# Output projections as split column halves, with columns of x turned between them, in a two-block language model

## The reference

```python
h = h + recurrent_block(...)      # ... return (y * hr) @ w_out
h = h + swiglu(h, ...)            # width 2816
h = h + nsa_layer(...)            # ... return o.reshape(B, S, N_HEADS * HEAD_DIM) @ w_out
h = h + swiglu(h, ...)
for layer in range(2):
    x = x + hybrid_mixer(rms_norm(x, ...), ...)   # return jnp.einsum('bsd,de->bse', y, w_out)
    x = x + swiglu_2(rms_norm(x, ...), ...) if layer % 2 == 0 else x + moe_swiglu(...)   # width 3584
return rms_norm(x, g)

def swiglu(h, norm_g, w_in, w_out):
    u = rmsnorm(h, norm_g)
    gu = u @ w_in
    return (jax.nn.silu(gu[..., :FFN_HIDDEN]) * gu[..., FFN_HIDDEN:]) @ w_out
```

## Time and profile before

| | us |
|---|---|
| median of 3 runs | 2581.16 (2578.05 to 2584.66) |
| the profiled execution | 2593.58 |
| its span in the trace | 2592.0 |
| PE busy (share of the span) | 2433.8 (94%) |
| DVE busy | 1652.1 (64%) |
| ACT busy | 1338.6 (52%) |

### The profile page before, as it was taken

One profiled execution on the slowest core, in us unless ns is written; L12 is line 12 of the kernel. 1 busy time (PEld: TensorE's weight loads), 2 busy tenths in 40 slices (PEclk: granted clock), 3 DMA queues, 4 the chain that ended last, 5 costly groups with the idle time before them and its releaser, 6 DMA issues.

```text
span 2592.0 us, 30679 instructions
## 1 busy us (share of the span) xinstructions
PE 2433.8 (94%) x12234; PEld 1975.8 (76%) x12234; DVE 1652.1 (64%) x1472; ACT 1338.6 (52%) x1184; POOL 58.6 (2%) x68
## 2 busy tenths in 40 slices
PE   7899998998998999899989988999999999999998
PEld 6488845767888896788789866777777877778876
DVE  5255535526546654555575557788878888888877
ACT  3244303425435663433457525666666667666765
POOL 0000010000000000000000001000000000000010
PEclk9999998999999999999999999999999999999999
DMA  6275363006553323555333237999999999999995
GB/s 217 82 259 194 132 229 114 1 17 240 180 182 106 131 98 130 195 194 194 138 130 130 98 138 286 348 358 357 356 345 357 368 363 362 368 354 374 369 375 213
DMA packets 251090, 588.53 MB, mean 227 GB/s; under 512 B 6476, under 2 KB 14864, under 8 KB 251008
## 3 DMA queue, kind: packets, MB, share of 16 engines
q1 hardware_dynamic: 244160, 564.27, 59.8%
q0 software_dynamic: 6656, 23.04, 2.4%
q10 hardware_dynamic: 192, 0.05, 0.0%
HBM read 573.19 MB, written 14.16 MB: 227 GB/s over the span
## 4 chain that ended last, share of the span: by engine, by line
PE 60%; DMA 16%; DVE 12%; ACT 9%; issue 2%; SPq 0%; ACTq 0%; DVEq 0%; PEldq 0%
DMA raw<-in_moe_w_gate 13%; PE ps L583 10%; PE ps L585 10%; PE ps L584 10%; DVE wl L1638 7%; PE ps L539 7%; ACT wh L1191 7%; PE ps L892 3%; PE ps L894 3%; PE ps L893 3%; DMA raw<-in_moe_w_down 2%; PE ps L531 2%; PE ps L838 1%; PE ps L794 1%; PE ps L779 1%
## 5 line engine op out<-in xcount | busy, mean ns | idle before, releaser
L1638 DVE TENSOR_TENSOR wl<-raw,wh 128x4096 fp32r<-128x4096 f32 (+1 forms) x221 | 968.9, 4386 | 246.6 <-ACT wh L1191 246.2
L1191 ACT ACTIVATE wh<-raw 128x4096 fp32r<-128x4096 f32 (+1 forms) x221 | 796.1, 3603 | 471.5 <-PE ps L585 187.5
L583 PE MATMUL ps<-wh,xmh 128*128 128x512 f32 x896 | 360.5, 402 | 34.2 <-DVE wl L1638 13.4
L584 PE MATMUL ps<-wl,xmh 128*128 128x512 f32 x896 | 352.7, 394 | 0.0
L585 PE MATMUL ps<-wh,xml 128*128 128x512 f32 x896 | 352.6, 394 | 0.0
L583 PE MATMUL ps<-wh,hh 128*128 128x512 f32 x712 | 279.5, 393 | 13.4 <-DVE hl L1653 13.3
L585 PE MATMUL ps<-wh,hl 128*128 128x512 f32 x712 | 278.0, 390 | 0.0
L584 PE MATMUL ps<-wl,hh 128*128 128x512 f32 x712 | 277.8, 390 | 0.0
L583 PE MATMUL ps<-wh,xh 128*128 128x512 f32 (+1 forms) x632 | 247.3, 391 | 17.5 <-issue 14.3
L584 PE MATMUL ps<-wl,xh 128*128 128x512 f32 (+1 forms) x632 | 243.1, 385 | 0.0
L585 PE MATMUL ps<-wh,xl 128*128 128x512 f32 (+1 forms) x632 | 243.1, 385 | 0.0
(11 more groups left out here) (477 smaller groups left out, 3378.4 us busy)
## 6 DMA issues: line engine op xcount, KB each, us to landing
raw<-in_moe_w_gate SPq DMA_DIRECT2D x56, 2048.0 KB, 9.7
raw<-in_moe_w_up SPq DMA_DIRECT2D x56, 2048.0 KB, 9.6
raw<-in_moe_w_down SPq DMA_DIRECT2D x56, 2048.0 KB, 9.5
raw<-in_w_in SPq DMA_DIRECT2D x22, 2048.0 KB, 8.0
raw<-in_f_w_in SPq DMA_DIRECT2D x20, 2048.0 KB, 8.4
raw<-in_f_w_out SPq DMA_DIRECT2D x10, 2048.0 KB, 8.1
raw<-in_dense_w_gate SPq DMA_DIRECT2D x7, 2048.0 KB, 7.7
raw<-in_dense_w_up SPq DMA_DIRECT2D x7, 2048.0 KB, 8.2
```

The source lines that it names most:

```text
L583: mm(ps[:, bank, 0:n], xa, a, start=(begin and k == 0), stop=False)
L584: mm(ps[:, bank, 0:n], xa, l, start=False, stop=False)
L1191: fn(wh[:, kind, 0:n], raw[:, s, 0:n], ACT.Copy).then_inc(wh_full[kind], 1)
L1638: v.tensor_tensor(wl[:, kind, 0:n], raw[:, plan[name][kind][0], 0:n], wh[:, kind, 0:n].bitcast(F32), ALU.subtract).then_inc(wl_full[kind], 1)
```

## The change

A new order for the four output products and what follows them:

- All four sites are split products in quarters of 256 columns, by one function (out_project on each engine). Sites 0 and 1 were full products. The banks of PSUM are 3, 4 and 5 (ring g), and wmo and ul have places in SBUF that live through all four sites.
- The operand of site 0 is made in halves: DVE multiplies, ACT copies to uh, DVE subtracts to ul. In the attention DVE copies each pair of heads to uh and subtracts it to ul, in place of the copy to oT.
- The first two quarters of the weights are split early: at site 0 between two evictions of ACT, and at site 1 in the first step of the attention.
- While a site multiplies quarter q + 1, DVE adds quarter q to x, and PE then turns these columns of x (turn_columns), which ACT and DVE split into xh and xl. The first gate and up tiles of the network behind it are split in between.
- The barriers in front of the three networks are gone. The first products of the network are ordered by k: four of gate's eight k, the last turn, and then the rest as the columns are ready; up is begun before gate ends where the tile has 256 columns.

Before, ACT had only the L1413 rows (then L1319) there. The diff, cut to what the steps need:

```diff
+                self.g = Ring([3, 4, 5], x_filled, x_added)
...
+        SITES = [(("a_out",), "ffn0", "f_norm", 0), (("b_out",), "ffn1", "f_norm", KD),
+                 (("mix_out", 0), "ffn2", "ffn_norm_2", 0), (("mix_out", 1), None, None, None)]
...
+            def natural(b, wh_, wl_):
+                for m in range(M):
+                    for k in range(KD):
+                        o, ms = ps[:, b, m * HW:(m + 1) * HW], slice(m * P, (m + 1) * P)
+                        mm(o, uh[:, k, ms], wh_[:, k, :], start=(k == 0), stop=False)
+                        mm(o, uh[:, k, ms], wl_[:, k, :], start=False, stop=False)
+                        t = mm(o, ul[:, k, ms], wh_[:, k, :], start=False, stop=(k == KD - 1))
+                return t
+            def turn_columns(site, q):
+                pe.wait_ge(x_added, 4 * site + q + 1)
+                b = me.s.claim(pe)
+                for kk_ in range(2):
+                    for m in range(M):
+                        t = tr(ps[:, b, (kk_ * M + m) * P:(kk_ * M + m + 1) * P],
+                               x[:, m, (2 * q + kk_) * P:(2 * q + kk_ + 1) * P], ident)
+                t.then_inc(s_filled, 1)
+            def out_project(site):
+                for q in range(4):
+                    me.see(mh_ready)
+                    me.see(ml_ready)
+                    b = me.g.claim(pe)
+                    natural(b, wmo[:, q % 2], out_view(site, q, raw_low)).then_inc(x_filled, 1)
+                    out_used[site, q] = (x_filled, me.g.n)
+                    if q % 2:
+                        released(out_key(site, q), me.g)
+                    if q and SITES[site][1]:
+                        turn_columns(site, q - 1)
...
-            me.see(yh_ready)
-            for t in range(2):
-                arrived(pe, ("a_out", t))
-                for m in range(M):
-                    product(me.v, ("a_out", t), m, rg)
-                released(("a_out", t), me.v)
             drained(me.v)
+            drained(me.a)
+            me.see(ul_ready, 2)
+            out_project(0)
...
-                norm(split="raw")
+                site = [s[1] for s in SITES].index(name)
+                def first_tile():
+                    def filled(kind):
+                        pe.wait_ge(wh_full[kind], B0 + 1)
+                        pe.wait_ge(wl_full[kind], B0 + 1)
+                    def split_columns(q):
+                        pe.wait_ge(s_read, me.s.n - 3 + q)
+                    filled(0)
+                    pe.wait_ge(s_read, me.s.n - 1)
+                    first_product(0, U0, w0, range(0, 4))
+                    turn_columns(site, 3)
+                    split_columns(2)
+                    first_product(0, U0, w0, range(4, 6))
+                    if w0 < FB:
+                        filled(1)
+                        first_product(1, U0, w0, range(0, 6))
+                    split_columns(3)
+                    first_product(0, U0, w0, range(6, KD)).then_inc(g_done, 1)
+                    if w0 == FB:
+                        filled(1)
+                    first_product(1, U0, w0, range(6 if w0 < FB else 0, KD)).then_inc(u_done, 1)
...
-            for t in range(2):
-                arrived(pe, ("b_out", t))
-                for m in range(M):
-                    product(me.v, ("b_out", t), m, oT)
-                released(("b_out", t), me.v)
-            drained(me.v)
-            me.barrier("ffn1")
+            drained(me.a)
+            drained(me.o)
+            out_project(1)
...
-                for t in range(2):
-                    for c in range(2):
-                        half_natural(me.v, Q_OUT + 2 * t + c)
-                    released(("mix_out", layer, t), me.v)
                 drained(me.v)
+                out_project(2 + layer)
...
+            def high_out(site, q):
+                arrived(act, out_key(site, q))
+                if q > 1:
+                    act.wait_ge(*out_used[site, q - 2])
+                fn(wmo[:, q % 2], out_view(site, q), ACT.Copy).then_inc(mh_ready, 1)
...
+            def high_columns(site):
+                b = me.s.take(act)
+                for kk_ in range(2):
+                    k = 2 * j + kk_
+                    t = fn(xh[:, k, :], ps[:, b, kk_ * S:(kk_ + 1) * S], ACT.Copy, scale=col(g, off + k))
+                t.then_inc(norm_h, 1)
+            def out_project(site):
+                name = SITES[site][1]
+                high_out(site, 2)
+                if not name:
+                    high_out(site, 3)
+                    return
+                nb, w0, B0, U0 = FFN[name]
+                high(name, 0, 0, U0, KD * w0)
+                high_columns(site)
+                high_out(site, 3)
+                high_columns(site)
+                high(name, 1, 0, U0, KD * w0)
...
+                if f in (3, 5):
+                    high_out(0, f // 2 - 1)
             act.wait_ge(a_read, me.a.n)
             act.nop().then_inc(yg_ready, 1)
+            for j in range(2):
+                me.see(yh_ready)
+                fn(uh[:, 4 * j:4 * j + 4, :], rg[:, 4 * j:4 * j + 4, :], ACT.Copy).then_inc(uh_ready, 1)
...
+            high_out(1, 0)
             probs(0, *pairs[0])
+            high_out(1, 1)
...
+            def low_out(site, q):
+                me.see(mh_ready)
+                v.tensor_tensor(out_view(site, q, raw_low), out_view(site, q), wmo[:, q % 2].bitcast(F32),
+                                ALU.subtract).then_inc(ml_ready, 1)
+            def add_columns(q):
+                b = me.g.take(dve)
+                xs = x[:, :, q * HW:(q + 1) * HW]
+                v.tensor_tensor(xs, xs, ps[:, b, :].rearrange("p (m n) -> p m n", m=M), ALU.add).then_inc(x_added, 1)
+            def low_columns(site):
+                b = me.s.take(dve)
+                me.see(norm_h)
+                for kk_ in range(2):
+                    k = 2 * j + kk_
+                    t = v.scalar_tensor_tensor(xl[:, k, :], ps[:, b, kk_ * S:(kk_ + 1) * S], col(g, off + k),
+                                               xh[:, k, :].bitcast(F32), ALU.mult, ALU.subtract)
+                t.then_inc(s_read, 1)
+            def out_project(site):
+                name = SITES[site][1]
+                add_columns(0)
+                low_out(site, 2)
+                if not name:
+                    add_columns(1)
+                    low_out(site, 3)
+                    add_columns(2)
+                    add_columns(3)
+                    return
+                nb, w0, B0, U0 = FFN[name]
+                n0 = KD * w0
+                low(name, 0, B0, n0)
+                low_columns(site)
+                add_columns(1)
+                low_out(site, 3)
+                low_columns(site)
+                add_columns(2)
+                if w0 < FB:
+                    low(name, 1, B0, n0)
...
+                add_columns(3)
+                low_columns(site)
+                low_columns(site)
+                if w0 == FB:
+                    low(name, 1, B0, n0)
...
-            link(v.tensor_tensor_scan(rg[:].rearrange("p k t -> p (k t)"), aa[:].rearrange("p k t -> p (k t)"),
-                                      ig[:].rearrange("p k t -> p (k t)"), 0.0, ALU.mult, ALU.add))
+            parts = [slice(0, KD // 2), slice(KD // 2, KD)]
+            for p_ in parts:
+                link(v.tensor_tensor_scan(rg[:, p_, :].rearrange("p k t -> p (k t)"), aa[:, p_, :].rearrange("p k t -> p (k t)"),
+                                          ig[:, p_, :].rearrange("p k t -> p (k t)"), 0.0, ALU.mult, ALU.add))
+            low_out(0, 0)
+            low_out(0, 1)
             me.see(yg_ready)
-            v.tensor_tensor(rg[:], rg[:], yg[:], ALU.mult).then_inc(yh_ready, 1)
-            for t in range(2):
-                for m in range(M):
-                    residual(t, m)
+            for p_ in parts:
+                v.tensor_tensor(rg[:, p_, :], rg[:, p_, :], yg[:, p_, :], ALU.mult).then_inc(yh_ready, 1)
+            for p_ in parts:
+                me.see(uh_ready)
+                v.tensor_tensor(ul[:, p_, :], rg[:, p_, :], uh[:, p_, :].bitcast(F32), ALU.subtract).then_inc(ul_ready, 1)
...
-                    v.tensor_copy(oT[:, h // 2, m * P:(m + 1) * P], ps[:, b, 0:P]).then_inc(o_read, 1)
+                    o = slice(m * P, (m + 1) * P)
+                    link(v.tensor_copy(uh[:, h // 2, o], ps[:, b, 0:P]))
+                    v.tensor_tensor(ul[:, h // 2, o], ps[:, b, 0:P], uh[:, h // 2, o].bitcast(F32),
+                                    ALU.subtract).then_inc(o_read, 1)
             me.scores_begin()
             maxima(0, *pairs[0])
+            low_out(1, 0)
+            low_out(1, 1)
...
-            po.wait_ge(stage, 3 * marks["ffn1"])
+            po.wait_ge(d_done, FFN_END["ffn1"])
```

178 lines of the change are left out of this document (74 added, 104 removed).

## The result

The changed kernel takes 2560.71 us (median of 4 runs, 2559.39 to 2569.71), the kernel before 2582.91 beside it (4 runs, 2578.05 to 2586.65). The ratio is 0.9921, 95% interval 0.9895 to 0.9947: 22.2 us faster. I had forecast 10.7 us less, 2570.5, with a range of 2563 to 2579, which the median misses by 2.3 us. In the two profiled executions the spans are 2592.0 and 2568.1 us, 23.9 apart. Two later sets gave ratios of 0.9905 (0.9875 to 0.9935) and 0.9916 (0.9882 to 0.9949).

What follows compares the result with a forecast made beforehand. Before 1550 us PE's chain of work plus its waits was taken to bound each stage. Savings of 5.0 (site 0), 2.3 (site 1 with attention) and 3.4 (site 2) make 10.7, off 2581.16: 2570.5 us, range 2563 to 2579.

Steps and rivals of the forecast that it cites:

- site 0, net of its later start: First product to first hb at site 0: 43.6 us falls to 33.5, less later start and half rate; 5.0 saved.
- site 1, entry: First product to first hb at site 1: 43.7 us falls to 33.5, less 0.9 for half rate; 9.3 saved.
- attention: first step, other heads, end: Attention before site 1: 4.2 us stall in first step, 2.5 in first-half heads, 0.3 behind last head; 7.0 lost.
- site 2: First product to first hb at site 2: 49.1 us falls to 45.7, half rate included; 3.4 saved (1.0 to 5.8).
- site 3: Last site, before the routing: order kept and the routing's barrier stays, so 0 us saved (within 0.3).
- half-rate terms: PE at 1.2 GHz after waits: 1.7 us at site 0's start, 0.9 each at sites 0 and 1, 2.4 at site 2.
- my sign of a wrong prediction: A stretch from the routing on differing by more than 3 us would make the prediction wrong.
- added subtraction: Attention's odd heads: copy plus dependent subtraction, 0.31 us more each; 2.5 in the first token half, 0 in the second.
- New waits: Rival, 25%: new waits eat the gain, each of three sites paying 2 us more; 4.7 us left, 2576.5.
- drain of 1.4 us: Rival, 2%: ACT drains at table switches; sites 0 and 1 lose 2.8 us each, site 2 1.4; 2577.5.
- Deeper gain: Rival, 16%: no half rate after short waits and heads absorb the added subtraction; about 15 us saved, 2566.
- the slower case: Rival, 5%: longer diagonal waits keep PE at 1.2 GHz in attention's first token half; some 19 us lost, 2589.

Runs made afterwards that it cites:

- after_wait: The changed kernel with 20 products ahead of site 3 whose result is thrown away (17.2 us in all); median 2575.49 us.
- The best version: The changed kernel with attention's early splits spread, site 0 begun on ul's first half, squares split, silu's table loaded behind the root; medians 2553.48 and 2552.51 us.
- before_ul: The kernel before with ul 128 bytes lower in SBUF, where the changed kernel has it; median 2576.67 us against 2584.55, ratio 0.9977.

## Why the prediction was wrong

The mechanisms were right in the main, and each size of the plan can be set beside its measurement, in us saved between the two profiled executions:

| step | forecast | measured |
|---|---|---|
| site 0, net of its later start | 5.0 | 6.1 |
| site 1, entry | 9.3 | 11.4 |
| attention: first step, other heads, end | -7.0 | -6.1 (-4.0, -1.7, -0.5, rounded) |
| site 2 | 3.4 | 5.0 |
| site 3 | 0 | 1.9 |
| rest of networks and mixers | 0 | -1.0 |
| routing to the end | 0 | 6.6 |
| sum | 10.7 | 23.9 |

- **The step that failed is the term put at nothing, "Site 3 keeps its order ... 0 (within 0.3)", and beside it the sizes of the terms for sites 0 to 2, all too low.** Site 3 gained 1.9 us in all three profiles. I took the order of instructions for all that counts, and passed over lines of the diff that move ul by 128 bytes. With ul moved back site 3 takes 30.7 us again, and with ul moved in the kernel before it takes 28.8; some 0.4 of the 1.9 us are the pace, the rest is the clock of the first quarter, which went with the place wherever nothing else had been changed ahead of site 3. Why it does is open. The place also made my quarters too dear: I took 0.120 us a product from rows of the old place, and it was 0.118, 0.4 us a site.
- **No single term carries the shortfall.** Up to the routing the forecast fell 6.5 us short (17.2 measured): site 1 by 2.1, site 3 by 1.9, site 2 by 1.6, site 0 by 1.1, the attention by 0.9, less 1.0 for the rest of networks and mixers. With site 3 at 1.9 the sum would have been 12.6 and the forecast 2568.6. The other two profiles have the routing 19.0 and 22.3 us earlier than before.
- **The half-rate terms were of the right kind and partly of the wrong size.** I charged sites 0 and 1 with 0.9 us each for the wait for silu; there PE lost none. Nor did it behind the waits inside site 2 (granted clock 1.00), for which I had 2.4. Ahead of the first quarters it did lose: at site 0, where I had 1.7, 27, 15 and 27 products ran at 1.2 GHz in the three profiles (2.6 and 1.4 us), and at site 2, where the rows of before held 1.7, 27 or none. The bounds held all of these; which value an execution takes is luck.
- **The stage of the experts was taken as equal.** "Differs by more than 3 us" from the routing on was my sign of a wrong prediction, and it came true (6.6). But this stage takes 1022.8 to 1036.2 in three profiles of one kernel, and arriving as late as before did not lengthen it (after_wait). The best version, with the new order and the new place of ul, took 1041.7, as long as before. In the medians it still seems shorter: 22 to 25 us of difference against 17 to 22 at the routing, and the two profiles of the old order have 1041.7 and 1039.2, where the fifteen of the new order have 1021.8 to 1041.7, 1031.7 in the mean. Whether some us of that have a cause stays open.
- **What held:** silu as the last releaser at sites 0 and 1; the waits of 1.49 and 2.77 us at site 2 (1.3 and 2.9); 4.0 us in the attention's first step (4.2); the barriers' removal cost nothing visible; the next tile of weights was in time (PE's later wait is 3.0 us, as in the earlier trace rows). From DVE's multiplication to PE's first product at site 0 it took 2.6 us longer in all three profiles (2.5 forecast), though the start itself came 0.7 to 3.4 us later, since what lies ahead of it varies.
- **What was right for another reason.** I had the added subtraction in the attention's first 16 heads (2.5 us) and none in the second 16. The first took 0.8 us longer (2.0 against before_ul) and the second 0.9, in all three profiles: the second half did not have the slack that I gave it.
- **The rivals.** New waits did not eat the gain: the margin before the fourth quarter at sites 0 and 1 held, and PE shows no wait there. The first half of the attention did not stay at 1.2 GHz: its granted clock was 0.90, as before (0.89). No drain of 1.4 us stands behind a table load: root and silu start 0.01 to 0.02 us after theirs. "Deeper gain" (2566) was the nearest, for a part of its reason: no half rate after the short waits. Its other half, heads that absorb the subtraction, was not so (1.7 us paid).
- **Slips in the sums.** A third of the growth of 57.6 us by 0.89 / 0.5 is 15 us and not 19, so the slower case lay at 2585.5, not at 2589, and under the bound of 2588.9; and site 2's lower end is 5.8 - 4.4 = 1.4, not 1.0. Neither moves the forecast or the range.

## What to carry to other kernels

Read a diff for what it moves in SBUF as well as for what it moves in time, and before an edit is credited with a gain, look at the pace of one instruction form that the edit should leave alone. When work is moved off a path, follow the next engine's chain to its end, table loads and the waits that stand ahead of them included: that chain gave the last 1.2 us of site 1. Where an edit changes how long an engine idles ahead of a stage, read more than one profile before the stage's time is credited to the edit. Keep a stage that waits for transfers out of the comparison of single profiles, and compare marks ahead of it.

## What the runs showed that I had not expected

- The place of one operand by 128 bytes sets the pace of float32r products with 256 columns, 0.1178 or 0.1198 us as a mean over the three products of a split one. Moving xh, xl and the hidden tiles took products with 512 columns from 0.2274 to 0.2321. The Trainium skill ("SBUF — State Buffer", section SBUF: two separate sides) says that of the engines only the pair that shares a port is in contention, and that PE never waits on anyone. These runs show that its pace still depends on where the operands lie, by 1.7% and 2%.
- The same wait of 1.64 us (1.65 in the first profile) ahead of site 2 was followed by 27 products at 1.2 GHz in one execution and by none in another of the same kernel.
- PE's first quarter at site 0 began at 2.4 GHz when four products filled the gap and left 1.02 us of it.
